# Identity products while the first rows arrive, a third tile with two banks of its own, and two tiles scaled on VectorE instead of GpSimd

## What is computed

```
rmsnorm(x, g):  x * rsqrt(mean(x*x) + 1e-6) * g
gq, gk, gv, glr, gg, pv, pg, fq, fk, fv, ff, fg = split(rmsnorm(h, norm_pre) @ w_in)
```

## Time and profile before

| | us |
|---|---|
| median of 3 runs | 696.24 (694.05 to 697.59) |
| the profiled execution | 691.88 |
| its span | 690.3 |
| PE busy in it | 653.8 (95%) |
| DVE, ACT, POOL busy | 391.0, 259.8, 150.6 |

### The profile page before, as it was taken

One profiled execution on the slowest core, in us unless ns is written; L12 is line 12 of the kernel. 1 busy time (PEld: TensorE's weight loads), 2 busy tenths in 40 slices (PEclk: granted clock), 3 DMA queues, 4 the chain that ended last, 5 costly groups with the idle time before them and its releaser, 6 DMA issues.

```text
span 690.3 us, 13168 instructions
## 1 busy us (share of the span) xinstructions
PE 653.8 (95%) x5145; PEld 562.0 (81%) x5145; DVE 391.0 (57%) x712; ACT 259.8 (38%) x479; POOL 150.6 (22%) x167
## 2 busy tenths in 40 slices
PE   4899999999999999999999989999999889999996
PEld 3889999898999889999999965766667655688884
DVE  5743926673455315159999967335443458654543
ACT  6537343111111245221112063745564557332321
POOL 3554112111111011223312040123222201121210
PEclk9999999999999999999999999999999999999999
DMA  8412103131100032344120282567666533123132
GB/s 229 144 43 62 32 1 75 32 92 31 32 11 23 5 84 80 83 159 123 30 62 1 82 254 88 159 168 218 182 199 191 171 140 107 41 67 122 61 123 91
DMA packets 59735, 67.29 MB, mean 97 GB/s; under 512 B 14156, under 2 KB 49883, under 8 KB 59673
## 3 DMA queue, kind: packets, MB, share of 16 engines
q1 hardware_dynamic: 54505, 51.37, 25.1%
q0 software_dynamic: 5168, 15.08, 7.4%
HBM read 57.71 MB, written 8.68 MB: 96 GB/s over the span
## 4 chain that ended last, share of the span: by engine, by line
PE 83%; DVE 8%; ACT 5%; issue 2%; POOL 1%; DMA 1%; SPq 0%; DVEq 0%; ACTq 0%; POOLq 0%
PE PS L1872 14%; PE PS L1873 13%; PE PS L1874 13%; PE PS L1775 4%; PE PS L1776 4%; PE PS L1777 4%; PE PS L2159 3%; PE PS L2141 3%; PE PS L2094 3%; PE PS L2116 2%; PE PS L2059 2%; PE PS L2046 2%; DVE rows_odd L1654 2%; DVE YF L1533 1%; PE PS L2185 1%
## 5 line engine op out<-in xcount | busy, mean ns | idle before, releaser
L1872 PE MATMUL PS<-xh,wh 128*128 128x368 f32 x576 | 196.3, 341 | 0.8 <-POOL wl L628 0.5
L1873 PE MATMUL PS<-xl,wh 128*128 128x368 f32 x576 | 190.3, 330 | 0.0
L1874 PE MATMUL PS<-xh,wl 128*128 128x368 f32 x576 | 189.9, 330 | 0.0
L628 POOL TENSOR_TENSOR wl<-wr,wh 128x1024 fp32r<-128x1024 f32 x24 | 61.7, 2570 | 262.9 <-ACT wh L1003 262.9
L1872 PEld LDWEIGHTS PS<-xh,wh 128*128 128x128 f32 x576 | 108.3, 188 | 4.9 <-issue 1.5
L1873 PEld LDWEIGHTS PS<-xl,wh 128*128 128x128 f32 x576 | 108.3, 188 | 0.9
L1874 PEld LDWEIGHTS PS<-xh,wl 128*128 128x128 f32 x576 | 108.3, 188 | 0.0
L609 DVE TENSOR_TENSOR wr<-wr,small 128x1024 f32<-128x1024 f32 x24 | 35.4, 1477 | 41.1 <-DMA wr<-in_w_in_dram 41.0
L1513 DVE RECIPROCAL RA<-RA 128x1104 f32<-128x1104 f32 x8 | 56.4, 7053 | 0.3
L1775 PE MATMUL PS<-woh,yh 128*128 128x512 f32 x128 | 50.6, 395 | 0.0
L1777 PE MATMUL PS<-woh,yl 128*128 128x512 f32 x128 | 50.3, 393 | 0.0
(11 more groups left out here) (325 smaller groups left out, 1118.4 us busy)
## 6 DMA issues: line engine op xcount, KB each, us to landing
wr<-in_w_in_dram SPq DMA_DIRECT2D x24, 512.0 KB, 3.8
kpage<-in_cache_fox_k_dram SPq DMA_DIRECT2D x64, 192.0 KB, 2.7
RA<-in_cache_fox_v_dram POOLq DMA_DIRECT2D x32, 192.0 KB, 3.5
pagesB<-in_cache_fox_v_dram POOLq DMA_DIRECT2D x32, 192.0 KB, 3.8
YF<-in_x_prompt_dram SPq DMA_DIRECT2D x8, 512.0 KB, 5.8
xres<-in_x_prompt_dram SPq DMA_DIRECT2D x8, 512.0 KB, 3.8
out_y_p_dram<-zout SPq DMA_DIRECT2D x16, 256.0 KB, 2.1
wo_raw_a<-in_w_out_dram SPq DMA_DIRECT2D x6, 512.0 KB, 5.0
```

The costliest lines, as they stand in the source:

```text
L628: eng.tensor_tensor(low, wr[:, c % 2, :, 0:m], wh[:, c % 2, :, 0:m].bitcast(F32), ALU.subtract).then_inc(wlo_done, 1)
L1872: pe.matmul(out, high, xh[:, k, cols], start=(k == 0), stop=False)
L1873: pe.matmul(out, high, xl[:, k, cols], start=False, stop=False)
L1874: ins = pe.matmul(out, low, xh[:, k, cols], start=False, stop=(k == KT - 1))
```

## The change

Four edits, all in the first stage. PE gets 19 products of the identity with itself, 128 columns each, written to a part of bank 3 that nothing has used yet: 10 ahead of the transposes of tile 0, 4 after them, 2 after those of tile 1 and 3 after those of tile 2. Tile 2 is transposed into banks 4 and 5 and no longer waits for `x_low(0)`; from tile 3 on the odd and even pairs of banks are exchanged, and tiles 3 and 4 wait for `x_low` of 0 and 1. ACT does `x_high(2)` ahead of the first half of `wh` instead of behind it. Tiles 4 and 6 are scaled on DVE, right behind tiles 3 and 5, and POOL scales tile 8 alone.

```diff
--- before.py
+++ after.py
@@ -102,7 +102,7 @@
 FIRST_COLS = [slice(0, NMETA + 2 * P), slice(NMETA + 2 * P, NMETA + 4 * P), slice(NMETA + 4 * P, NMETA + 6 * P),
               slice(NMETA + 6 * P, NT)]
 FIRST_ROWS = [3, 5, 7, 9]
-SCALED_DVE, SCALED_POOL = [0, 1, 2, 3, 5, 7], [4, 6, 8]
+SCALED_DVE, SCALED_POOL = [0, 1, 2, 3, 4, 5, 6, 7], [8]
 SQUARED_ACT, SQUARED_DVE = [0, 1, 2, 3, 4, 5, 7], [6, 8]
 
 
@@ -576,12 +576,20 @@
 
         XORDER = [NTILE] + list(range(NTILE))
 
+        def x_bank(i):
+
+            return 4 if i == 2 else (1, 6)[i % 2] if i > 2 else (6, 1)[i]
+
+        def x_before(i):
+
+            return {3: 0, 4: 1}.get(i, i - 2)
+
         def x_halves(i):
 
             t = XORDER[i]
             for half in range(2):
                 ks = slice(4 * half, 4 * half + 4)
-                src = PS[:, (6, 1)[i % 2] + half, :].rearrange("p (k t) -> p k t", t=P)
+                src = PS[:, x_bank(i) + half, :].rearrange("p (k t) -> p k t", t=P)
                 yield 2 * i + half + 1, [(src[:, :, r0:r1], (slice(0, P), ks, slice(col, col + r1 - r0)))
                                          for r0, r1, col in xcols(t)]
 
@@ -852,7 +860,7 @@
             w_scale(g, 0)
             for i in SCALED_POOL:
                 t = XORDER[i]
-                g.wait_ge(refined, SCALED_POOL.index(i) + 1)
+                g.wait_ge(refined, i // 2 - 1)
                 g.tensor_scalar(xrows[:, t, :], xrows[:, t, :], rstd[:, t:t + 1], refine[:, t:t + 1],
                                 ALU.mult, ALU.mult).then_inc(xs_pool, 1)
             link(g.memset(pool_w[:, :, :], 0.0))
@@ -1012,9 +1020,9 @@
             x_roots(2, 1)
             x_high(0)
             x_high(1)
+            x_high(2)
             act.wait_ge(wg_half, 1)
             act.activation(wh[:, 1, 0:4, :], wr[:, 1, 0:4, :], ACT.Copy).then_inc(whi_half, 1)
-            x_high(2)
             w_high(1)
             w_high(0)
             x_squares(3)
@@ -1288,18 +1296,24 @@
                 link(dve.tensor_scalar(f, f, -0.5, 1.5, ALU.mult, ALU.add))
 
 
+            def refine_two(i):
+                t = XORDER[i]
+                r, f = rstd[:, t:t + 2], refine[:, t:t + 2]
+                dve.wait_ge(rms_done, 3 + (i - 1) // 2)
+                link(dve.reciprocal(r, r))
+                link(dve.tensor_tensor(f, f, r, ALU.mult))
+                link(dve.tensor_tensor(f, f, r, ALU.mult))
+                dve.tensor_scalar(f, f, -0.5, 1.5, ALU.mult, ALU.add).then_inc(refined, 1)
+
             def x_scale(i):
                 t = XORDER[i]
                 m = n_of(t)
-                dve.wait_ge(rms_done, SCALED_DVE.index(i) + 1)
                 if i < 3:
+                    dve.wait_ge(rms_done, i + 1)
                     rsqrt(rstd[0:m, t:t + 1], refine[0:m, t:t + 1])
                 else:
-                    r, f = rstd[:, t:t + 2], refine[:, t:t + 2]
-                    link(dve.reciprocal(r, r))
-                    link(dve.tensor_tensor(f, f, r, ALU.mult))
-                    link(dve.tensor_tensor(f, f, r, ALU.mult))
-                    dve.tensor_scalar(f, f, -0.5, 1.5, ALU.mult, ALU.add).then_inc(refined, 1)
+                    if i % 2:
+                        refine_two(i)
                     dve.wait_ge(refined, (i - 1) // 2)
                 dve.tensor_scalar(xrows[0:m, t, :], xrows[0:m, t, :], rstd[0:m, t:t + 1], refine[0:m, t:t + 1],
                                   ALU.mult, ALU.mult).then_inc(xs_done, 1)
@@ -1338,10 +1352,12 @@
             w_low(dve, 1)
             w_low(dve, 0)
             x_scale(3)
+            x_scale(4)
             x_squares(6)
             x_low(3)
             x_low(4)
             x_scale(5)
+            x_scale(6)
             lf_rest(0)
             x_squares(8)
             x_low(5)
@@ -1782,11 +1798,11 @@
                 m = n_of(t)
                 x_scaled(pe, i)
                 for half in range(2):
-                    if i >= 2:
-                        pe.wait_ge(xlo_done, 2 * (i - 2) + half + 1)
+                    if i >= 3:
+                        pe.wait_ge(xlo_done, 2 * x_before(i) + half + 1)
                     for n_ in range(4):
                         k = 4 * half + n_
-                        ins = pe.transpose(PS[:, (6, 1)[i % 2] + half, P * n_:P * n_ + m], xrows[0:m, t, P * k:P * k + P],
+                        ins = pe.transpose(PS[:, x_bank(i) + half, P * n_:P * n_ + m], xrows[0:m, t, P * k:P * k + P],
                                            ident[0:m, 0:m])
                     ins.then_inc(xt_full, 1)
 
@@ -1835,12 +1851,22 @@
                 if t == 3:
                     ins.then_inc(in_full, 1)
 
+            def keep_busy(n):
+
+                for _ in range(n):
+                    pe.matmul(PS[:, 3, 0:P], ident[:, :], ident[:, :], start=True, stop=True)
+
             def first_chunks():
 
                 pe.wait_ge(d_gpre, 16)
                 pe.transpose(PS[:, 5, 0:KT], gpre_rows, ident[0:KT, 0:KT]).then_inc(gpre_full, 1)
-                for i in range(3):
-                    x_transposes(i)
+                keep_busy(10)
+                x_transposes(0)
+                keep_busy(4)
+                x_transposes(1)
+                keep_busy(2)
+                x_transposes(2)
+                keep_busy(3)
                 first_chunk(0)
                 low_rank(0)
                 x_transposes(3)
```

## The result

| | before | after |
|---|---|---|
| median, 7 runs each | 694.05 us | 690.7 us |
| ratio, 95% interval | | 0.9947 (0.9925 to 0.9970) |
| the profiled execution | 691.88 us | 691.41 us |
| its span | 690.3 us | 689.8 us |
| first product of `project_in(2)` | 45.72 us | 42.09 us |

The kernel is 3.7 us faster by the ratio (2.1 to 5.2). The last line of the table is what I compare from here on and call the stage. It starts at DVE's first scaling (8.10 before, 7.64 after), because the first rows land up to half a microsecond earlier or later.

The account below looks back on a forecast made before the run. PE, busy 95% of the span, was taken as the bound. `project_in(2)` starting 2.3 us earlier (45.72 to 43.4) turns 691.88 into 689.6 us; plus 4.36 to the median gives 693.9 us, range 691.3 to 697.3.

Parts of the forecast that it names:

- Where the time is: Whole change lies ahead of `project_in(2)`, whose first product starts at 45.72 us; all behind moves with it.
- The sign and the engine: Faster by 2.3 us, by shortening PE's list or filling its holes; PE is busy 95% of the span.
- the absolute time: Profiled execution 691.88 becomes 689.6 us; adding the 4.36 us by which the median lay above it gives 693.9.
- The price of an identity product: Each of PE's 19 products priced as a transpose: 0.21 us at the lower clock, 0.12 at the higher.
- the moment of the rise: PE's clock goes to its higher level at 12.3 us, ahead of tile 1's last transposes, saving 1.9 us at block 0.
- the 0.35 us that I charged to tile 1: Four products between tiles 0 and 1 end at 10.95; tile 1 could start at 10.61, so 0.35 us late.
- a case in which the rise before is usually later than in the profile shown: Early clock rise then saves up to 1.9 us more; chance 0.18 of measuring faster.
- The two scalings: Tiles 4 and 6 take 0.81 us each on DVE, against POOL's 2.79 and 3.14; transposes 5 and 6 end 2.35 us earlier.
- The banks: Tile 2 in banks 4 and 5, with ACT's new order: block 0 starts at 15.05 instead of 15.35, 0.3 us.
- the rival that rested on it: Transposes do not count, PE's clock rises at 19.1 as before; gain 0.5 us, 695.7 us; chance 0.28.
- The slower rival: PE's clock rises only after block 0, which starts at 16.3; 2.0 us slower, 698.2 us; chance 0.10.
- Late rise: PE's clock rises only at about block 0's start; gain 1.0 to 1.3 us, 695.1 us; chance 0.20.

Follow-up runs that it names:

- e6: Changed kernel with tiles 4 and 6 scaled on POOL again, all 19 products and the new banks kept; ratio to the kernel before 0.9983, stage 36.90 us.
- e3: Changed kernel with only the ten products ahead of tile 0, the 4, 2 and 3 deleted; ratio to the kernel before 0.9966, stage 34.61 us.
- e10: Kernel before with only tile 2 in banks 4 and 5 and ACT's first half of `wh` behind `x_high(2)`; ratio 0.9995, stage 37.95 us.
- e7: Changed kernel with the old banks and ACT's old order, products and DVE's scalings kept; ratio to the kernel before 0.9955, stage 35.56 us.
- e1: Changed kernel without its 19 identity products, profiled twice; ratio to the kernel before 0.9971, stages 36.29 and 38.32 us.
- e9: Kernel before with only tiles 4 and 6 scaled on DVE; ratio to the kernel before 0.9996, stage 35.76 us.
- e5: Changed kernel with 18 identity transposes ahead of tile 0 in place of all 19 products, profiled twice; ratio to before 0.9969, stages 36.05 and 34.85 us.

## Why the prediction was wrong, step by step

- *Where the time is: right.* The whole gain lies ahead of `project_in(2)`, and what is behind moves with it to 0.1 us (644.6 us in both kernels) where no fall of the clock comes in between.
- *The sign and the engine: right.* The clock at block 0 and the scalings moved off POOL carry it.
- *The step that failed, larger part: the absolute time.* I carried 4.36 us from the profiled execution to the median of three runs. With seven runs the kernel before has 694.05, 2.17 us above that execution; 30 runs beside the second profile have 694.31. On 694.05 the same forecast would read 691.75. The profiled execution has no fall of the clock behind the stage; of the kernel's runs a third (10 of 29) to three fifths (18 of 30) have one. So of the 3.2 us between 693.9 and 690.7, 2.2 are this term, and the rest is about what the gain was forecast too small by.
- *The price of an identity product: wrong.* I took 0.21 us at the lower level and 0.12 at the higher; measured are 0.43 and 0.225. I read "x4" in the earlier trace rows as four products where it is two, each entered twice; read so, they give 0.24 for a third of the columns. In the profile shown it cost nothing, because the ten end at 8.50 and tile 0 is scaled at 8.45. In the second they end at 8.94, half a microsecond behind the scaling, and even so tile 1 is transposed as soon as it is scaled (10.50 and 10.55). In e6, with its later rise, the four behind tile 0 end 0.9 us after tile 1 is scaled.
- *The step that failed, smaller part: the moment of the rise.* I put it at 12.3; it was at 7.8, and at 8.8 in the second profile. The ten products, which I had taken to end at 6.9 with a hole behind them, ran without a hole up to tile 0, and by e3 they alone do it. My reason, that the holes between the tiles had kept the clock low, is not borne out (e10, and the second and third profile of before). So the 0.35 us that I charged to tile 1 did not exist. Behind the first scaling (forecast against measured, the first profile): block 0 at 6.95 and 6.66, its end 10.0 and 9.8, block 1 at 15.05 and 14.65, `low_rank(1)` at 20.3 and 19.34, the first product of `project_in(2)` at 35.3 and 34.45. ACT's squares of tile 3 come 0.6 us earlier than I had them, DVE's list with them, and DVE's lateness of 0.35 us at tile 5 (forecast 26.45 against PE ready at 26.1) never arises. That is 0.9 us: 3.2 gained in the stage where I forecast 2.3.
- *The spread that I priced and then left small.* I gave 1.9 us to a case in which the rise before is usually later than in the profile shown, at 0.18. The other two profiles of before have stages longer by 0.9 and 0.7. That is not a later rise (15.6 and 19.4 against 19.3) but tile 1, scaled 1.1 and 0.95 us later behind tile 0, which can hit the changed kernel too. How often it does in unprofiled runs stays open.
- *The two scalings: right.* 0.8 us each on DVE; by e6 worth 2.3 us given the rest, of which 1.8 arise behind block 0.
- *The banks: sign right, size small.* 0.3 us forecast, 0.4 to 0.55 by e7, counted from tile 1. What I had not seen is that the new banks also take a hole out of the transposes.
- *Do transposes count?* The page "TensorE: Matmul & The Clock Gate" of the Trainium skill, part 4, has transposes not counting as busy. Here the clock rose at 8.4 and 9.5 us behind 18 transposes, where before it was low until 15.6 at the earliest: the measurement decides against the rule, and the rival that rested on it (0.28) fell.
- *The slower rival* did not come for the changed kernel, but its mechanism is real: the second look at e1 has no rise before the end of block 0 (22.2) and a stage of 38.32.
- *Late rise*: the last nine alone (stage 35.71, a gain of 1.9) come nearest to it.

Whether the parts add is open. Alone, the products give 1.7 us by the ratio, the banks and the scalings 0.3 each with intervals across zero, 2.3 in sum; together 3.4 to 3.7. The intervals would allow a plain sum, and e9's falls hide part of what its edit gives. Why the parts may help each other is argued from the stages, not shown: with the clock high PE meets POOL's scalings early and waits, with DVE's scalings and a low clock it is block 0 that takes the time.

## What to carry to other kernels

Where PE idles for rows at the start, fill that hole with products up to the moment of the first real work, and read the speed of the first real instructions (0.62 us for eight transposes against 1.1) to see whether it worked; in e3 and e6 these were still slow and the rise came just behind them. Speeding up one engine pays only if the next supplier is moved as well: here the holes that POOL left cost time themselves. Take the time that a forecast is tied to from many runs, and more than one profile of the kernel before. Before two profiles are compared, look whether the same data landed at the same time, and compare unprofiled runs of like mean granted clock.

## What the runs showed of the hardware

- The page's clock row reads 9 and the windows 1.00 over 4 to 14 us of the changed kernel, where a product took 0.43 us at first and 0.225 later. The trace's records of the granted clock begin only at the first rise (7.8 us there, 19.3 before), and the views print 1.00 ahead of it. The first low stretch has to be read from starts. Later falls are shown (0.50 between 26 and 28 us in the second profile of before).
- A plain float32 product of 128x128 by 128 columns takes 0.43 us at the lower level (0.44 on average over ten, e3) and 0.225 at the higher, and has two entries in the trace; a transpose of the same size takes 0.21 and 0.11 and has one.
- The clock rose with nothing but float32 transposes ahead of it (e5, 18 of them and tile 0's, at 8.4 and 9.5 us).
- The clock held through holes of 1.35 us (ahead of block 0 in e3) and fell behind one of 1.79 (e5). Behind holes of 0.94 and 0.74 it fell once (before, second profile) and held once (e6, 0.95 and 0.74).
- On one core, in the middle of dense work, some executions of either kernel have the clock at half for some microseconds near 240 us: mean 0.65 and 0.67 in two windows of 5 us, for 3.1 us of time. The trace shows where (`after`), not why:

```profile
235.00:240.00 5.00, 5.00 (x27) 0.65 0.00 0
240.00:245.00 5.00, 5.00 (x22) 0.67 0.37 64
```
